# Head norms over few columns, routing scores in row halves among the expert units, and a block inverse in 64x64 quarters

## The reference, cut to what matters

```python
ada = silu(c) @ w_ada + b_ada               # 12 pieces of 512 columns; sh1, sc1, g1, sh2, sc2, g2
h = modulate(rmsnorm(x, norm1_g), sh1, sc1)
gate_b, gate_c, xa, xr, gr = split(h @ w_in)
xr = causal_dwconv(xr, conv_b_w) + conv_b_b # 4 taps, then the recurrence rg_lru
y = concat([head_rmsnorm(y_a, gn_a, 8), head_rmsnorm(y_b, gn_b, 8)]) @ w_out   # mean over 64 wide heads

# peer: routing of each token to experts
q = (xb @ w_q).reshape(p, 8, 2, 64)
sc = einsum('phcd,hcnd->phcn', q, sub_keys) # 8 heads, 2 halves of 64 rows, 128 keys
top_s, top_i = top_k(sc, 16)                # ... and the experts' dense products over all 16384

# second block: gated delta rule, 4 heads of 128
a = where(strict, (k_beta @ k.T) * decay, 0)
t_inv = triangular_solve(a + eye, eye)      # unit lower triangular
```

## Time and profile before

| | us |
|---|---|
| median of 3 runs | 1985.86 |
| profiled execution, its own time | 1983.03 |
| its span, first to last instruction | 1981.3 |
| PE busy / PEld busy | 1834.3 / 1581.7 |
| DVE / POOL / ACT busy | 1620.6 / 1054.1 / 708.5 |
| mean granted clock of PE | 0.967 of full speed |

### The profile page before, as it was taken

How to read it: one execution, slowest core, us unless ns; L and a number is a source line. 1 busy time by engine, 2 the same in 40 slices (tenths; PEclk the granted TensorE clock), 3 DMA queues, 4 the chain that set the end, 5 groups by cost and what they waited for, 6 DMA issues and landing times.

```text
span 1981.3 us, 27281 instructions
## 1 busy us (share of the span) xinstructions
PE 1834.3 (93%) x9487; PEld 1581.7 (80%) x9487; DVE 1620.6 (82%) x2566; ACT 708.5 (36%) x1097; POOL 1054.1 (53%) x654
## 2 busy tenths in 40 slices
PE   3997779999999999999999999999999998989885
PEld 1775557999999899999988887878887776778764
DVE  6979967978988798888489999999998868747656
ACT  2343123333333444444333333333334333324441
POOL 1333225488888655555567776767765542343101
PEclk8999779999999999999999999999999999999988
DMA  8241342499889789888999999999994222200011
GB/s 344 88 159 64 128 149 74 137 315 315 308 314 314 258 280 325 300 308 299 317 348 356 353 356 353 349 356 351 363 352 146 75 77 63 73 12 1 2 55 52
DMA packets 160805, 440.34 MB, mean 222 GB/s; under 512 B 13648, under 2 KB 63952, under 8 KB 157648
## 3 DMA queue, kind: packets, MB, share of 16 engines
q1 hardware_dynamic: 65296, 254.71, 36.7%
q0 software_dynamic: 36864, 134.23, 17.9%
q10 hardware_dynamic: 58560, 50.34, 7.7%
HBM read 386.80 MB, written 52.43 MB: 222 GB/s over the span
## 4 chain that ended last, share of the span: by engine, by line
PE 68%; DVE 18%; issue 4%; POOL 4%; ACT 3%; DMA 2%; ACTq 0%; SPq 0%; DVEq 0%; POOLq 0%; PEldq 0%
PE PS L911 30%; PE PS L1078 24%; PE PS L1041 4%; PE PS L1104 4%; POOL w_lo L804 3%; DVE arena L1676 2%; DVE arena L1635 2%; DVE arena L1842 1%; ACT w_hi L1277 1%; PE PS L926 1%; POOL arena L852 1%; PE PS L1002 1%; DMA arena<-in_expert_u_rows,arena 1%; DMA xres<-in_x 1%; DVE arena L1774 1%
## 5 line engine op out<-in xcount | busy, mean ns | idle before, releaser
L804 POOL TENSOR_TENSOR w_lo<-raw,w_hi 128x1024 fp32r<-128x1024 f32 x300 | 725.0, 2417 | 757.7 <-ACT w_hi L1277 756.5
L1277 ACT ACTIVATE w_hi<-raw 128x1024 fp32r<-128x1024 f32 x332 | 351.9, 1060 | 973.4 <-PE PS L911 609.7
L911 PE MATMUL PS<-act_hi,w_hi 128*128 128x384 f32 (+1 forms) x1632 | 603.9, 370 | 37.3 <-DVE act_lo L1648 12.2
L911 PE MATMUL PS<-act_hi,w_lo 128*128 128x384 f32 (+1 forms) x1632 | 588.4, 361 | 0.0
L911 PE MATMUL PS<-act_lo,w_hi 128*128 128x384 f32 (+1 forms) x1632 | 587.5, 360 | 0.0
L911 PEld LDWEIGHTS PS<-act_hi,w_hi 128*128 128x128 f32 x1632 | 311.8, 191 | 91.7 <-issue 25.3
L911 PEld LDWEIGHTS PS<-act_lo,w_hi 128*128 128x128 f32 x1632 | 312.0, 191 | 26.4
L911 PEld LDWEIGHTS PS<-act_hi,w_lo 128*128 128x128 f32 x1632 | 312.6, 192 | 24.3 <-issue 1.4
L1078 PE MATMUL PS<-w_hi,act_hi 128*128 128x512 f32 x768 | 301.3, 392 | 5.6 <-ACT arena L1398 3.0
L1078 PE MATMUL PS<-w_lo,act_hi 128*128 128x512 f32 x768 | 300.2, 391 | 0.0
L1078 PE MATMUL PS<-w_hi,act_lo 128*128 128x512 f32 x768 | 299.9, 390 | 0.0
(11 more groups left out here) (317 smaller groups left out, 1962.7 us busy)
## 6 DMA issues: line engine op xcount, KB each, us to landing
raw<-in_expert_u SPq DMA_DIRECT2D x128, 512.0 KB
raw<-in_expert_v SPq DMA_DIRECT2D x128, 512.0 KB
raw<-in_w_in SPq DMA_DIRECT2D x52, 512.0 KB
arena<-in_w_ada SPq DMA_DIRECT2D x24, 1024.0 KB, 7.1
gel_d<-arena ACTq DMA_DIRECT2D x64, 384.0 KB
gates_d<-arena ACTq DMA_DIRECT2D x12, 2048.0 KB
arena<-gates_d SPq DMA_DIRECT2D x32, 768.0 KB, 7.1
arena<-gel_d SPq DMA_DIRECT2D x32, 768.0 KB
```

The lines of the kernel that those rows point to most:

```text
L804: pool.tensor_tensor(w_lo[:, k % SPLIT, :], raw[:, k % RAW, :], w_hi[:, k % SPLIT, :].bitcast(F32), ALU.subtract).then_inc(lo_split, 1)
L911: mm = pe.matmul(PS[:, bank, 0:n_tok], w[:, k % SPLIT, c * P:(c + 1) * P], x[:, c, 0:n_tok], start=(i == 0 and n == 0), stop=(i == KC - 1 ...
L1277: act.activation(w_hi[:, k % SPLIT, :], raw[:, k % RAW, :], ACT.Copy).then_inc(hi_split, 1)
```

## The change

Three parts, and some smaller moves around them.

*Head norms.* The sum of squares is now taken with the squares as the stationary operand and two columns as the moving one, so a tile's 512 tokens x 2 heads are 128x8 numbers. Root and reciprocal work on these. ACT then repeats each number over 64 columns (`spread`), PE turns the result with 4 products against the identity (`head_spread`), and DVE scales y from PSUM.

*Front.* For pieces 2 and 3 of the condition DVE adds up 4 chunks of 8 and PE does the other 4 (`PE_SHARE`); POOL begins its first low part after the fourth piece; pieces 4 and 5 come later on both engines; the 4-tap convolution keeps its partial sums in PSUM.

*Scores.* Keys are held without zeros, each score is four products of 64 rows by 128 columns; the fourth comes after the last `w_q` unit and the other twelve after each of the first 12 expert units (`N0`), which are unrolled. The keys' memory is moved so that it may live on; two pairs of row buffers share a semaphore (`landed`).

*Inverse.* `Dm` and `DTm` are block diagonal with 64x64 blocks until level 6, so levels 0 to 5 hold both quarters in 64 columns per head (`Dq`), with products of 64x64 (`quarters`). Level 6 is one quarter per product, and has no masks.

```diff
+            def head_sum(i):
...
+                pair = halves[:, :].rearrange("p (a b) -> p a b", a=2)[:, :, 0]
+                for q in range(TB):
+                    mm = pe.matmul(PS[:, 6 + index % 2, 2 * q:2 * q + 2], sq[:, n % 2, q * P:(q + 1) * P], pair,
+                                   start=True, stop=True)
...
+            def head_spread(i):
+                pe.wait_ge(spread_ready, i + 1)
+                if i >= 2:
+                    pe.wait_ge(y_scaled, i - 1)
+                for q in range(TB):
+                    mm = pe.matmul(PS[:, 3 + i % 2, q * P:(q + 1) * P], tmp[:, i % 2, q * P:(q + 1) * P], ident[:, :],
+                                   start=True, stop=True)
+            def head_root(i):
+                act.wait_ge(sum_ready, 2 + i)
...
+                act.activation(hrms[:, i % 2, :], PS[:, 6 + (1 + i) % 2, 0:8], ACT.Sqrt, bias=eps,
+                               scale=1.0 / 64).then_inc(rms_ready, 1)
+            def spread(i):
+                act.wait_ge(rinv_ready, 2 + i)
...
+                act.activation(tmp[:, i % 2, :].rearrange("p (a b) -> p a b", b=64),
+                               hinv[:, i % 2, :].unsqueeze(2).to_broadcast([P, 8, 64]), ACT.Copy).then_inc(spread_ready, 1)
+                v.reciprocal(hinv[:, i % 2, :], hrms[:, i % 2, :]).then_inc(rinv_ready, 1)
             def scale_y(i):
-                v.scalar_tensor_tensor(out=y[:, c, :], in0=y[:, c, :], scalar=col("gn", c), in1=rinv, op0=ALU.mult,
-                                       op1=ALU.mult).then_inc(y_scaled, 1)
+                v.scalar_tensor_tensor(out=y[:, c, :], in0=y[:, c, :], scalar=col("gn", c), in1=PS[:, 3 + i % 2, :],
+                                       op0=ALU.mult, op1=ALU.mult).then_inc(y_scaled, 1)
-        Y_SCALE = (13, 16, 17, 18, 19, 20, 20, 20)
+        Y_INV = (13, 16, 17, 18, 19, 20, 20, 20)
+        Y_SPREAD = (17, 18, 19, 20, 20, 20, 20, 20)
             def ada_half(h):
+                if h in PE_SHARE:
...
+                    for n in range(4):
+                        for c in range(4, KC):
...
+                            mm = pe.matmul(PS[:, 5, own:own + 1], ada_w[:, (2 * h + 1) % 4, at:at + P], cs[:, c:c + 1],
+                                           start=(c == 4), stop=(c == KC - 1))
-                for c in range(KC):
+                for c in range(4 if h in PE_SHARE else KC):
+            pool.wait_ge(ada_acc, 4)
             for u in range(U_Q):
                 lower(u, u)
-            pool.memset(keys[:, :, :], 0.0).then_inc(pool_made, 1)
+            pool.nop().then_inc(pool_made, 1)
-        SCORED_AFTER = {2: 0, 4: 1, 6: 2}
-        ADA_AFTER = {3: 4, 5: 5, ...
+        SCORED_AFTER = {2: 0, 4: 1, 6: 2, 7: 3}
+        N0 = 12
+        PE_SHARE = (2, 3)
+        ADA_AFTER = {5: 4, 7: 5, ...
-                    mm = pe.matmul(PS[:, 3 + n % 2, 256 * e:256 * e + 256], qT[:, 2 * hp + e, tb * P:(tb + 1) * P],
-                                   keys[:, 2 * hp + e, :], start=True, stop=True)
+                    for c in range(2):
+                        own = slice(64 * c, 64 * c + 64)
+                        mm = pe.matmul(PS[:, 3 + c, P * e:P * e + P], qT[own, 2 * hp + e, tb * P:(tb + 1) * P],
+                                       keys[own, 2 * hp + e, :], start=True, stop=True)
-            for n in range(len(SCORED_AFTER), TB * 4):
-                scores(n)
+            for u in range(N0):
+                if u >= 2:
+                    pe.wait_ge(gelu_done, u - 1)
+                linear(U_EU + u, u, u % 2, n_tok=TD)
+                scores(len(SCORED_AFTER) + u)
+            def quarters(name, *pieces):
+                b = bank(*name)
+                wait_free(pe, *name)
+                for h in range(GH):
+                    for to, lhs, rhs in pieces:
+                        mm = pe.matmul(PS[to, b, 64 * h:64 * h + 64], lhs[:, h, :], rhs[:, h, :], start=True, stop=True)
+                full(mm, *name)
-                        heads(("x", n, tb), lambda h: h4(DTm[:, tb, :])[:, h, :], lambda h: h4(M1[:, tb % 2, :])[:, h, :])
-                    heads(("xt", n, tb), lambda h: h4(M1[:, tb % 2, :])[:, h, :], lambda h: h4(DTm[:, tb, :])[:, h, :])
+                        quarters(("x", n, tb), *((own, turned_inverse(tb)[own], m1[own]) for own in (LO, HI)))
+                        quarters(("xt", n, tb), *((own, m1[own], turned_inverse(tb)[own]) for own in (LO, HI)))
+                    else:
+                        quarters(("xt", n, tb), (LO, m1[HI], h4(DTm[:, tb, :])[HI, :, HI]))
-                    chain.post(v.tensor_tensor(DTm[:, tb, :], DTm[:, tb, :], PS[:, bank("xt", n, tb), :], ALU.subtract))
+                    d, dt = Dq[:, tb, 0:256], Dq[:, tb, 256:512]
+                    turned_x = PS[:, bank("xt", n, tb), 0:256]
+                    if n < LEVELS - 2:
+                        chain.post(v.tensor_tensor(dt, dt, turned_x, ALU.subtract))
```

211 lines of the change are left out of this document (146 added, 65 removed).

## The result

The changed kernel takes 1971.85 us, the median of 4 runs (1969.61 to 1973.12); the kernel before took 1985.62 in 4 runs beside it. The ratio is 0.9928, interval 0.9911 to 0.9945: faster by 0.7%, where 2.3% was forecast. 1971.85 lies outside the range of 1925 to 1957. The profiled execution has a span of 1971.4 us against 1981.3, so 9.9 us less.

A forecast was written before the change was run, and what follows sets the result against it. PE bounds the expert stages and the inverse, DVE the front and output units. Gains of 23.3 us (front, head norms), 1 (scores) and 20 (inverse) sum to 44, giving 1941 from 1985.9; predicted 1940, range 1925 to 1957.

The forecast's parts named there:

- The forecast's own sign of being wrong: Weighted(6) starting after 200, or a level of the inverse at 14 us or more, would make the prediction wrong.
- PE's share of the condition: Front: PE takes half the chunks of pieces 2 and 3 at 3.8 us each; norm starts 4.6 us earlier.
- POOL's hold on DVE: Front: POOL's low parts hold DVE's norm until about 40.8; gain 4.6 us, without the hold 7.
- Pieces 4 and 5: Front: moved to where DVE idles, removing PE's 1.46 us wait and 1.66 of low clock: 3.1 us.
- The input units: Head norms: PE's 3.86 us wait goes, last unit at full clock, two turned products come in: gain 3.4 us.
- The tail: From the last input unit's end to weighted(6): 16.5 us in place of 28.7, bounds 12 and 28.7.
- Rival B: Head-norm tail is a chain of latencies, rounds keep 5.44 us; total time 1954 us, chance 0.10.
- Carry it on unchanged: Output units, norm 2 and w_q units pass on the 23.3 us gained at weighted(6) without loss.
- The scores: Score about 0.65 us; 0.9 and 8.2 won, 7.8 lost among expert units; took 1 us, bounds 3.9 and -1.9.
- The inverse: Quarter jobs 0.55 us, two engines near 11 give levels of 12 for 15.6; five levels gain 18 us.
- Together 20: Inverse: 18 us from five levels plus 2 from level 6 and level 0; bounds 6 and 30.
- The rivals: Quarters not paying 0.13, latency-chain tail 0.10, both ends freer 0.14, slower 0.04, little effect 0.03.

The follow-up runs named there:

- e6_burst12: Changed kernel with the twelve scores put back in one row behind w_q, in their new form; 1967.82 us, ratio 0.9897.
- e3_noshare: Changed kernel with DVE adding up all 8 chunks of pieces 2 and 3 of the condition; 1980.74 us, ratio 0.997.
- e11_best: e5_tail plus e7_burst4's scores, one identity copy per block, PE taking 2 chunks of piece 3, and two small edits not tried alone; 1947.65 us, ratio 0.9804.
- e1_early: Changed kernel with ACT spreading the first four inverse roots a unit earlier, ahead of the weights' high part; 1956.98 us, ratio 0.9849.
- e5_tail: e1_early with tile 6's square and sum a unit earlier and tail sums and spreads reordered; 1952.74 us, ratio 0.9826.
- e7_burst4: Changed kernel with four more scores put behind w_q and eight left between the first expert units; 1964.45 us, ratio 0.9893.

## Why the prediction was wrong

44.3 us were forecast up to the first unit behind the inverse and 9.6 came. The steps that failed, by what they missed: the order around the head norms 15.8 (10.1 in the input units, 5.7 in the tail), the inverse 9.0, the clock in the front 4.3, the scores 3.8, what was to be carried on unchanged 1.7; the rest is under 1 us each. The forecast's own sign of being wrong, weighted(6) after 200, is met with 213.25; the level, at 13.2, stays under its 14.

**PE's share of the condition.** The failed step: "at 1.92 us for 8 products (16 records) that is 3.8 us each", "PE stays busy there, so the four sums after it should cost 0.95". I took for granted that a busy PE keeps the clock. Measured: 6.56, 6.96 and 1.85, at a granted clock of 0.50 with PE busy 4.00 us of 4.00. The price itself was right for the full clock (3.7 by the starts in e6_burst12); only the clock was wrong. That is 4.3 of the 4.6 us, and no rival had it.

**POOL's hold on DVE** was right, though in the changed kernel it decided nothing: e3_noshare and e11_best show 3.45 and 3.38 us for instructions of 1.42. The rule of the Trainium skill ("SBUF — State Buffer", "SBUF: two separate sides") agrees with both. The row at 36.11, which I took as the sign of it, has one large operand and not two, so it was weaker evidence than I made of it.

**Pieces 4 and 5**: 3.5 us against 3.1, right.

**The input units.** "The 3.86 us wait goes ... two of the turned products ... come in: 3.9 + 1.1 - 2.0 = 3.0". The wait went, but the turned product brought its own. I counted what the new instructions cost PE and not what they stand behind on ACT. From unit 17 to the last unit's end 6.7 us were lost in place of 3.4 won; e1_early shows that it was this order: with the spread first, that end lies at 180.6, 10.6 us earlier.

**The tail.** "In-order waits ... add about 4: I walked the order ... and come to 16.5." It took 22.1. Rival B had the mechanism, a chain of latencies; the rounds fell from 5.44 only to 4.53. The ring runs through PE's order (a sum behind a turned product) and ACT's (a spread behind the root of that sum), and while PE idles in it the granted clock is 0.50, at which a turned product takes 2.07 in place of 1.0 and a sum 1.71 in place of 0.95. That 13.1 us are to be had (e5_tail) says that the sizes in the forecast were fair, and that this order was not.

**"Carry it on unchanged"** for the units up to w_q's end: 3.6 became 1.85. 1.1 of it is in the last three output units, which take 19.36 us in place of 18.22: the clock is low from 250.0 to 256.9, before from 255.5 to 259.0. The three scores between w_q units saved 0.3 together, not 0.9.

**The scores.** Price 0.65 right as a product (0.64), wrong as a step between units (0.85): the forecast charged no change of tile shape here, though it quoted the rule of the Trainium skill ("TensorEngine Tiling (Array Packing)", "Key Properties") for the inverse. 8.2 won, 11.0 lost over twelve units: 10.2 is the price, 1.5 the first unit at the low clock, less 0.8 of waits in units 10 and 11 that only the kernel before has. So -2.8 in place of +1, below the lower bound of -1.9.

**The inverse.** The mechanism was right: jobs 0.54 (0.55 forecast), PE 11.0 us a level (10.8), DVE 10.2 (10.9). Two terms were mis-sized. "Two engines at 11, in order, give 12": they gave 13.2. And "Together 20": level 0, level 6 and the setting up were counted as a gain of 2 and were a loss of 3.3: 1.65 ahead of the first copy (1.1 of it memsets, while the copies on half of the rows saved nothing) and 1.66 behind the first copy of level 6, at the low clock. 11.0 in all.

The rivals were weighed as if one could fail at a time. Each term was near the middle of its own range; most came out at the lower end, because they lean on the same two things, PE's clock and in-order waits.

## What to carry to other kernels

When work is moved to an engine "with room", ask first what it stands behind in that engine's order and what that waits for: here a 0.6 us spread behind a 1.06 us high part took back all that was won by shrinking eight reciprocals of 3.35. Where PE's work gets smaller or narrower, price it at both clocks, and the work around it too. A wait that an edit removes is worth its length only after the new order has been followed once around the ring of engines.

## What was not expected of the hardware

- PE busy without a gap with float32 products of one column, or of 64, was granted 0.50 of full speed; products started 0.22 us apart at full clock and 0.43 at half.
- A DVE copy on 64 rows of 512 columns took 0.416 us, on 128 rows 0.414.
- Eight 64x64x64 products took 0.54 us when quarters alternated and 0.67 when they did not; four of 128x128x128 took 0.98.
- The steps before and behind a score, where the tile shape changes, are 0.1 us longer each. That the change of shape is the cause is not shown by a run of its own.
- Four scores put into a gap of PE kept the granted clock at 1.00 (e7_burst4); with the gap left empty it was 0.50 for 6.8 us behind it.
- With the same code in the front the clock fell between 27.6 and 29.8 us, and the norm started at 45.0 to 45.4 in some executions and at 42.0 to 42.2 in others: a profile alone would have credited that to an edit.
